# Square roots on ScalarE's logarithm table, sums taken one unit later, and attention's value products three steps back

## The reference, cut to what matters

```python
hx = rms_norm(x, norm_g[l]) * (1.0 + scale) + shift
px = split_cols(hx @ w_in[l])
attn = windowed_attention(q, k, v, kc, vc, attn_sink[l])   # 8 heads of 64, window 128, plus 256 context keys
y = mixer_out(attn, px, ...)                               # attention, convolution, Fourier; times silu(gates); @ w_out
x = x + gate * y
```

## Time and profile before

| | |
|---|---|
| median of 3 runs | 4803.69 us |
| profiled execution | 4812.23 us |
| its span | 4810.5 us |
| busy: PE, PEld, DVE, ACT, POOL | 82%, 66%, 54%, 33%, 24% |
| mean granted TensorE clock | 0.918 |

### The profile page before, as it was taken

How to read it: one execution, slowest core, us unless ns; L and a number is a source line. 1 busy time by engine, 2 the same in 40 slices (tenths; PEclk the granted TensorE clock), 3 DMA queues, 4 the chain that set the end, 5 groups by cost and what they waited for, 6 DMA issues and landing times. The chain is left out here.

```text
span 4810.5 us, 50758 instructions
## 1 busy us (share of the span) xinstructions
PE 3938.7 (82%) x18774; PEld 3170.7 (66%) x18774; DVE 2603.4 (54%) x3476; ACT 1604.0 (33%) x2643; POOL 1159.9 (24%) x969
## 2 busy tenths in 40 slices
PE   4658998688697899868868779999998867776997
PEld 0546886566375688666646558877887656664776
DVE  2634953688365495358845663340000469995554
ACT  2232102577221210157722122232111655553331
POOL 0421110122021121012202011111110048884443
PEclk7778999899898899989989889999999989997999
DMA  4333122321364312132126431123211355554443
GB/s 186 116 100 110 70 79 78 100 53 49 117 212 142 113 70 79 70 102 56 49 95 212 144 133 69 74 92 115 77 71 64 124 145 151 143 138 157 169 168 107
DMA packets 315775, 529.45 MB, mean 110 GB/s; under 512 B 26878, under 2 KB 203670, under 8 KB 299608
## 3 DMA queue, kind: packets, MB, share of 16 engines
q1 hardware_dynamic: 276970, 353.85, 23.7%
q0 software_dynamic: 38592, 172.82, 9.6%
HBM read 373.59 MB, written 153.00 MB: 109 GB/s over the span
## 5 line engine op out<-in xcount | busy, mean ns | idle before, releaser
L455 PE MATMUL in_ps<-h,in_wp 128*128 128x512 f32 x6624 | 1509.9, 390 | 18.6 <-POOL in_wp L618 18.5
L455 PEld LDWEIGHTS in_ps<-h,in_wp 128*128 128x128 f32 x6624 | 1247.6, 188 | 280.9 <-POOL in_wp L618 21.4
L1660 PE MATMUL out_ps<-out_y,out_wp 128*128 128x512 f32 x3072 | 731.4, 400 | 84.1 <-ACT out_y L1550 34.7
L1660 PEld LDWEIGHTS out_ps<-out_y,out_wp 128*128 128x128 f32 x3072 | 590.7, 193 | 225.3 <-issue 70.0
L588 DVE SCALAR_TENSOR_TENSOR cy<-cu,in_cw,cy 128x2048 f32<-128x2048 f32 x120 | 314.5, 2621 | 4.3
L1593 POOL TENSOR_TENSOR out_wp<-out_w,out_wp 128x2048 fp32r<-128x2048 f32 (+1 forms) x48 | 192.8, 4017 | 439.0 <-ACT out_wp L1539 438.9
L516 ACT ACTIVATE in_ob<-in_ps 128x2048 f32<-128x2048 f32 x37 | 69.7, 1884 | 663.8 <-PE in_ps L455 663.8
L1003 DVE TENSOR_TENSOR att_pT<-att_T,att_pT 128x512 fp32r<-128x512 f32 x320 | 221.1, 691 | 91.0 <-ACT att_pT L928 87.3
L618 POOL TENSOR_TENSOR in_wp<-in_w,in_wp 128x1024 fp32r<-128x1024 f32 x75 | 201.7, 2691 | 252.7 <-ACT in_wp L466 217.1
L1919 DVE TENSOR_SCALAR hi_z<-hi_z 128x4 f32<-128x4 f32 x1 | 0.2, 173 | 462.4 <-ACT hi_z L1876 462.4
L982 DVE CUSTOM_DVE_ANT_0 att_S<-att_S,att_mk,att_nsink 128x640 f32<-128x640 f32 x256 | 226.2, 884 | 27.0 <-PE att_S L851 26.1
(11 more groups left out here) (493 smaller groups left out, 6599.1 us busy)
## 6 DMA issues: line engine op xcount, KB each, us to landing
in_w<-in_w_in SPq DMA_DIRECT2D x75, 512.0 KB, 3.6
gates<-in_ob POOLq DMA_DIRECT2D x36, 1024.0 KB, 4.2
out_w<-in_w_out SPq DMA_DIRECT2D x32, 1024.0 KB, 4.9
out_mw<-in_w_ada_rows SPq DMA_DIRECT2D x48, 512.0 KB, 3.8
att_qf<-q SPq DMA_DIRECT2D x64, 256.0 KB, 4.3
out_yr<-y SPq DMA_DIRECT2D x16, 1024.0 KB, 7.5
x<-out_x POOLq DMA_DIRECT2D x64, 256.0 KB, 3.6
out_yr<-y SPq DMA_DIRECT2D x32, 512.0 KB, 5.7
```

Of the source, the lines that this page charges most:

```text
L455: mm = nc.tensor.matmul(ps[:, q, c * W:(c + 1) * W], wp[:, q, i, k], h[:, j, k, c * W:(c + 1) * W], start=(n + k == 0), stop=(n == 2 and k ...
L1660: mm = nc.tensor.matmul(ps[:, u % NB, :W], wp[:, u % NW, a, k], y[:, c % 2, b, k], start=(i + k == 0), stop=(i == 2 and k == KY - 1))
```

## The change

Four edits go together.

1. In `modulations` and `project_out` the reciprocal root is no longer a square root on ACT and a reciprocal on DVE, but two ACT instructions, `Ln` and `Exp` with scale -0.5, on a table set that holds both and is loaded once ahead of the loop.
2. In `project_out` without `last_gain` (out, outc) the accumulator of squares is doubled. PE's sums move from after unit n = 0 to after n = 1, the root to n = 2, the second root to n = 3, the store of the row to n = 4; DVE's part is cut in pieces that stand behind `gather` (`mean_again`, `both_roots`). `out_2` keeps its places.
3. The tile for the modulation rows (`mw`) goes from two buffers to one: SP issues the load for unit u only once DVE has finished with unit u-1's. DVE does the dot products ahead of `gather`, not behind. The residual loads run one unit further ahead.
4. In `attention` LAG goes from 2 to 3 and the ring of rounded tiles `pT` from 4 to 6.

```diff
 def modulations
+            nc.scalar.preload_act_table_set("natural_log_exp_and_others")
...
-                    nc.scalar.activation(rs[:, a % 2, 0:W], psR[:, a % 2, 0:W], ACT.Sqrt, bias=eps[:, 0:1]).then_inc(rooted, 1)
+                    nc.scalar.activation(rs[:, a % 2, 0:W], psR[:, a % 2, 0:W], ACT.Ln, bias=eps[:, 0:1]).then_inc(rooted, 1)
+                    act.wait_ge(rooted, a + 1)
+                    nc.scalar.activation(rs[:, a % 2, 0:W], rs[:, a % 2, 0:W], ACT.Exp, scale=-0.5).then_inc(inverted, 1)
...
-            for a in range(len(chunks) - 1):
+            for a in range(len(chunks)):
                 sums(a)
-                invert(a)
-            sums(len(chunks) - 1)
             for m in range(n_sets):
                 mods(m)
-            invert(len(chunks) - 1)
 def attention
-    SL, LAG = max(NH, U), 2
+    SL, LAG, RING = max(NH, U), 3, 6
...
-                wait(act, summed, m - 3)
+                wait(act, summed, m - RING + 1)
 def project_out
+    NA = 1 if last_gain else 2
+    SUM_AT, ROOT_AT, AGAIN_AT, ROW_AT = (0, 0, 0, 1) if last_gain else (1, 2, 3, 4)
...
             def modulation(j):
-                wait(sp, dotted, (j - 1) * m_n)
-                sp.dma_start(mw[:, j % 2], m_w[j]).then_inc(mw_in[j % 2], 16)
+                wait(sp, dotted, j * m_n)
+                sp.dma_start(mw[:], m_w[j]).then_inc(mw_in, 16)
...
                 if not base:
-                    residual(u)
-                if later and 0 <= u - LEAD + 1 < NJ:
-                    modulation(u - LEAD + 1)
+                    for v in range(2 * u, 2 * u + 2) if u < 1 else (u + 1,):
+                        if v < U:
+                            residual(v)
+                if later and 0 <= u - LEAD < NJ:
+                    modulation(u - LEAD)
...
+            nc.scalar.preload_act_table_set("natural_log_exp_and_others")
             for u in range(U):
...
-                if n == 0 and c:
+                if n == ROOT_AT and c:
                     root(c - 1)
+                if middle and n == AGAIN_AT and c:
+                    root_again(c - 1)
                 square(u)
...
-                if n == 0 and c:
+                if n == SUM_AT and c:
                     sums(c - 1)
...
-                if n == 0 and c:
-                    finish(c - 1)
+                if last_gain and n == 0 and c:
+                    scale_out(c - 1)
                 for a in ahead(u):
                     piece(*a)
                 add(u)
-                gather(u)
                 if later and 0 <= u - LEAD < NJ:
                     modulation(u - LEAD)
                 if later and u - LEAD == NJ:
                     modulations_done()
+                gather(u)
+                if middle and n == ROOT_AT and c:
+                    mean_again(c - 1)
+                if middle and n == AGAIN_AT and c:
+                    both_roots(c - 1)
```

More of the change, by code:

```diff
@@ L926, in heads @@
                 act.wait_ge(turned, n + 1)
[L927 to L928 removed]
+                wait(act, summed, m - RING + 1)
+                nc.scalar.activation(pT[:, m % RING, 0], psT[:, n % 2], ACT.Copy).then_inc(led, 1)
             def cross(b, g):
@@ L1557, in root, with root_again @@
                     wait(act, row_out, 16 * c * (2 if middle else 1))
-                nc.scalar.activation(rs[:], ps[:, S1, :W], ACT.Sqrt, bias=eps[:, 0:1]).then_inc(rooted, 1)
-                if middle:
-                    act.wait_ge(chain, 3 * c + 2)
-                    nc.scalar.activation(tm[:], tm[:], ACT.Sqrt, bias=eps[:, 0:1]).then_inc(rooted, 1)
+                nc.scalar.activation(rs[:], ps[:, S1, :W], ACT.Ln, bias=eps[:, 0:1]).then_inc(logged, 1)
+                act.wait_ge(logged, ROOTS * c + 1)
+                nc.scalar.activation(rs[:], rs[:], ACT.Exp, scale=-0.5).then_inc(rooted if middle or last_gain else finished, 1)
+            def root_again(c):
+                act.wait_ge(chain, 2 * c + 2)
+                nc.scalar.activation(tm[:], tm[:], ACT.Ln, bias=eps[:, 0:1]).then_inc(logged, 1)
+                act.wait_ge(logged, 2 * c + 2)
+                nc.scalar.activation(tm[:], tm[:], ACT.Exp, scale=-0.5).then_inc(rooted, 1)
             def square(u):
@@ L1627, in _ @@
                     store(u)
-                if row_d is not None and u >= KT and u % KT == 1:
+                if row_d is not None and u >= KT and u % KT == ROW_AT:
                     row(u // KT - 1)
@@ L1644, in sums @@
                 wait(pe, finished, c)
-                mm = nc.tensor.matmul(ps[:, S1, :W], ones[:], acc[:, 0], start=True, stop=True)
+                mm = nc.tensor.matmul(ps[:, S1, :W], ones[:], acc[:, c % NA, 0], start=True, stop=True)
                 if middle:
-                    mm = nc.tensor.matmul(ps[:, S2, :W], ones[:], acc[:, 1], start=True, stop=True)
+                    mm = nc.tensor.matmul(ps[:, S2, :W], ones[:], acc[:, c % NA, 1], start=True, stop=True)
                 mm.then_inc(summed, 1)
@@ L1706, in gather @@
                 else:
                     if middle:
-                        stt(acc[:, 1], ps[:, SQ, :W], g2[:, n:n + 1], acc[:, 1], ALU.mult, ALU.add)
-                    tt(acc[:, 0], acc[:, 0], ps[:, SQ, :W], ALU.add).then_inc(gathered, 1)
-            def finish(c):
-                dve.wait_ge(rooted, (2 * c if middle else c) + 1)
-                if not middle:
-                    if last_gain is None:
-                        nc.vector.reciprocal(rs[:], rs[:]).then_inc(finished, 1)
-                        return
-                    nc.vector.reciprocal(rs[:], rs[:]).then_inc(inverted, 1)
-                    dve.wait_ge(inverted, c + 1)
-                    for n in range(KT):
-                        x = xb[:, c % NX, n]
-                        ins = stt(x, x, last_gain[:, n:n + 1], rs[:], ALU.mult, ALU.mult).then_inc(finaled, 1)
-                    dve.wait_ge(finaled, (c + 1) * KT)
-                    dve.sem_inc(finished, 1)
-                    return
-                nc.vector.reciprocal(rs[:], rs[:]).then_inc(inverted, 1)
-                dve.wait_ge(inverted, c + 1)
+                        stt(a[:, 1], ps[:, SQ, :W], g2[:, n:n + 1], a[:, 1], ALU.mult, ALU.add)
@@ new lines, in gather, with scale_out, mean_again @@
+                    tt(a[:, 0], a[:, 0], ps[:, SQ, :W], ALU.add).then_inc(gathered, 1)
+            def scale_out(c):
+                dve.wait_ge(rooted, c + 1)
+                for n in range(KT):
+                    x = xb[:, c % NX, n]
+                    ins = stt(x, x, last_gain[:, n:n + 1], rs[:], ALU.mult, ALU.mult).then_inc(finaled, 1)
+                dve.wait_ge(finaled, (c + 1) * KT)
+                dve.sem_inc(finished, 1)
+            def mean_again(c):
+                dve.wait_ge(rooted, 2 * c + 1)
```

45 lines of the change are left out of this document (24 added, 21 removed).

## The result

The changed kernel takes 4759.8 us, median of 4 runs (4748.0 to 4763.5), against 4805.1 for the kernel before beside it (4802.8 to 4810.6): a ratio of 0.990, 95% interval 0.988 to 0.992, so about 45 us less. I had forecast 4714 with a range of 4688 to 4748. The direction is right, the size is half of what I wrote.

The account below looks back on a forecast made before the run. PE was nearly full in attention, as were DVE and ACT, but held back by waits in `out`. Terms -31 - 24 + 2 - 29 - 6 - 2 = -90 took 4812.2 to 4722, with the median 8.5 lower: 4714 us, range 4688 to 4748.

Parts of the forecast that it names:

- Modulations, -31: First stage: without the reciprocal on DVE the chain of input loads becomes the limit, last root at 99.3; -31 us.
- Attention, -24: Attention, both layers: waits change with LAG 3, a block takes 18.8 us, 0.8 less; -24 us, the term trusted least.
- The bound of +15: Attention: upper bound on the change in us, if each turn costs half a microsecond more.
- a clock below 0.90: Sign of being wrong: TensorE clock below 0.90 where PE now waits less; no chance given.
- Output projection, layer 0, +2: `out` of layer 0: the single-buffer loop's cost slightly exceeds savings; +2 us, bounds -3 and +11.
- The loop of 6.35 us a unit: `out` of layer 0: row load, then two dot products in series, 6.35 us per unit against DVE's 4.3 before.
- Output projection, layer 1, -29: `out` of layer 1: PE's waits for sums and input pieces go, PE sets the pace; -29 us, bounds -34 and -20.
- `out_2`, -6: `out_2`: table load and reciprocal leave the path, so scaling comes earlier; -6 us.
- my bounds of -4 and -8: `out_2`: the limits in us set around the forecast of -6.
- the three turns: `out_2`: earlier scaling gives back POOL's waits before its stores, 1.7 + 0.9 + 0.9 us.

Follow-up runs that it names:

- the two repeats: Changed kernel, fourth head's attention scores moved after their step's transposes and computed three times, filling TensorE's wait: 4700.6 us.
- the repeats elsewhere: Changed kernel, transposes first in that step, but the seventh head's scores repeated twice, where PE has no wait: 4767.0 us.
- The two-buffer kernel: Changed kernel with two modulation row buffers in layer 0's output projection, conditions kept in bf16 to make room: 4743.2 us.
- the fastest one: Changed kernel with both the fourth head's scores repeated twice and two row buffers in layer 0's output projection: 4691.5 us.

## Why the prediction was half right

**Modulations, -31.** Right, step by step: -30.6 in the trace, -29.6 in the kernel with this edit alone. Without the reciprocal on DVE the stage ends with the chain of input loads, and the last root is within 0.5 us of the figure.

**Attention, -24.** The step that failed. The working was right: the wait at the first value product grows (2.0 forecast, 1.77 measured), the second nearly goes, and the block takes 18.8 us (18.9 measured in the undisturbed turns). What I did not do was to lay the waits of the new turn beside PE's clock. I carried the clock of 1.00 over from the turns of the kernel before, where the waits stood apart, and moved them next to each other. The clock then falls in most turns, and 20.45 - 18.9 = 1.55 us a turn turns -24 into +19 (25 falls make 39). That idle time is a cause and not a companion is shown by the two repeats: 56 turns in two kernels without a fall, and attention 41 us shorter with more work in it, some 26 of them by the repeats themselves. Idle time is not all of it, as the spared turns in layer 1 of the repeats elsewhere show. With the clock held, attention is 9.3 and 12.5 us shorter than before, -22 in all: the forecast was that of a kernel with a clock it did not have. The bound of +15 for "half a microsecond more a turn" was too small as well, since it came from no mechanism. I had named a clock below 0.90 as a sign of being wrong, and gave it neither a rival nor a price.

The Trainium skill (TensorE: Matmul & The Clock Gate, "HAM oscillation — how this bites in real kernels") describes a wait that recurs in each pass and makes the clock fall each time. The traces agree in part: 12 and 13 falls in 14 turns each, none with work in the wait, but also none in the kernel before, whose waits recur as well; and the longest wait of a turn is 1.77 us here, shorter than in the section's example. The section was one to weigh in the prediction.

**Output projection, layer 0, +2.** Measured -0.2. The loop of 6.35 us a unit is there (DVE's dot products start at 1360.66, 1366.84, 1373.10, 6.2 apart), and PE waits 7.48 and 6.86 us for the sums. The two-buffer kernel shows that the loop is the bound: without it the stage is 17.3 us shorter. The change had turned DVE's long `finish` into a wait for a row, at no net cost.

**Output projection, layer 1, -29.** Measured -30.5. Of PE's waits for sums and input pieces, 0.43 us at one turn and the 2.92 at the end remain. With one dot product a unit the single buffer is hidden, as worked out.

**`out_2`, -6.** Measured -1.2, outside my bounds of -4 and -8. The end came as forecast: from the last sums to the end of the kernel 19.1 us against 22.1, -2.9 where I had -2.7. From the stage's first matmul to the first sums it took 1.4 us more (122.5 against 121.1), where no instruction was changed. What failed are the three turns, forecast at -3.5: from sums to sums PE takes 96.6 and 96.4 us against 96.1 and 96.7, no gain. I had read POOL's waits before its stores (2.00, 1.16, 1.16) as time that an earlier scaling gives back. Timelines of POOL and DVE at the second turn, before and after:

```profile
4611.52 4.61 POOL L1593 TENSOR_TENSOR out_wp<-out_w,out_wp 128x2048 fp32r<-128x2048 f32 x1 [6.27 <-ACT out_wp L1539]
4615.34 5.98 DVE L1721 SCALAR_TENSOR_TENSOR out_x<-out_x,final_g,out_rs 128x512 f32<-128x512 f32 x8
4617.29 5.16 POOL L1598 DMA_DIRECT2D out<-out_x  x8 [1.16 <-DVE out_x L1721]
```
```profile
4565.94 4.60 POOL L1603 TENSOR_TENSOR out_wp<-out_w,out_wp 128x2048 fp32r<-128x2048 f32 x1 [6.26 <-ACT out_wp L1539]
4567.03 8.70 DVE L1726 SCALAR_TENSOR_TENSOR out_x<-out_x,final_g,out_rs 128x512 f32<-128x512 f32 x8 [10.94 <-ACT out_rs L1560]
4571.69 5.16 POOL L1608 DMA_DIRECT2D out<-out_x  x8 [1.16 <-DVE out_x L1726]
```

DVE begins to scale 2.7 us earlier after the sums, but the eight instructions take 8.70 us instead of 5.98, and POOL's stores start 8.1 us after the sums (4609.17 and 4563.59) in both kernels. The group of the scaling before and after shows where the time sits, in the longest single instruction:

```profile
L1721 DVE SCALAR_TENSOR_TENSOR out_x<-out_x,final_g,out_rs x32: 733/744/1337, 4520.7 to 4798.5; 128x512 f32<-128x512 f32 x32
```
```profile
L1726 DVE SCALAR_TENSOR_TENSOR out_x<-out_x,final_g,out_rs x32: 737/740/4057, 4470.4 to 4749.8; 128x512 f32<-128x512 f32 x32
```

The first scaling instruction takes 4.06 us in each turn: it starts at 4567.03 and ends at about 4571.1, 0.55 after POOL's instruction (4570.54). Before, the reciprocal of 3.35 us stood there beside POOL's split and was not held up, and the scaling came after the split in the first turn (held by nothing) and just ahead of its end in the other two (held to 1.34 us). So removing the reciprocal brought the last scaling forward by 0.9 us in the first turn (12.1 us after the sums against 13.0) and by nothing in the next two (12.1 in both kernels); and the 0.9 did not reach PE, which waited 5.13 us behind that turn before and 5.54 after. What came last there is the load of the next chunk's residual, for which DVE waited 8.04 us before and 9.29 after. The Trainium skill (SBUF — State Buffer, "SBUF: two separate sides") has the pair of ports that VectorE and GpSimd share as an exclusive lock, which a VectorE instruction with two inputs from SBUF has to wait for; the trace agrees, with 4.06 us. No run here moved POOL's split away, so this is read and not tested.

## What to carry to other kernels

When a change moves waits on TensorE, list them in order with the work between them and ask whether the clock that you carry over still holds: shorter waits in sum, closer together, cost 19 us here where the same schedule with TensorE kept busy won 22. A price taken from an instruction's usual duration also needs a look at what its new neighbours are; a 0.7 us VectorE instruction took 4.06 beside one of GpSimd. And a wait that is needed anyway can be filled with repeated work that writes the same values to a place no one reads yet.

## What the runs showed of the hardware

- The granted clock fell in 21 of 28 turns whose longest wait was 1.16 us and held in all turns of the kernel before with 1.39, so the longest wait is no measure for it. A fall lasted 3.4 us in nearly all turns, at times 6.8.
- Two turns with the same instructions and waits can differ: 18.9 us at clock 1.00 and 20.45 with a fall, in one execution. The repeats elsewhere spread most from run to run, 53 us between the fastest and the slowest; the other kernels show no order by falls (15 us for the changed kernel, and 15 for the fastest one, which has none).
- A VectorE `SCALAR_TENSOR_TENSOR` of 0.74 us that began during a GpSimd `TENSOR_TENSOR` took 4.06 us and ended 0.55 us after it, in all three turns of `out_2`; a VectorE reciprocal of 3.35 us beside the same GpSimd instruction kept its length.
